# Ten instead of nine of 22 group products by seven multiplications in each half of a down projection

## The reference

```python
hf = rms_norm(x, norm_ffn)
gate, up = jnp.split(hf @ w_gu, 2, axis=-1)
return x + (jax.nn.silu(gate) * up) @ w_down      # [256 x 5632] @ [5632 x 2048]
```

## Time and profile before

| | before |
|---|---|
| time, median of 3 runs | 1106.16 us (1105.78 to 1106.39) |
| profiled execution | 1106.36 us, span 1104.6 us |
| TensorE matmul busy | 1092.2 us (99%), 5115 instructions |
| VectorE busy | 863.2 us (78%) |
| ScalarE busy | 580.2 us (53%) |
| down projection | about 865 to 1095 us of the span |
| granted TensorE clock | 0.997 of full speed on average |

### The profile page before, as it was taken

How to read it: one execution, slowest core, us unless ns; L and a number is a source line. 1 busy time by engine, 2 the same in 40 slices (tenths; PEclk the granted TensorE clock), 3 DMA queues, 4 the chain that set the end, 5 groups by cost and what they waited for, 6 DMA issues and landing times.

```text
span 1104.6 us, 13920 instructions
## 1 busy us (share of the span) xinstructions
PE 1092.2 (99%) x5115; PEld 908.8 (82%) x5115; DVE 863.2 (78%) x1057; ACT 580.2 (53%) x704; POOL 41.1 (4%) x70
## 2 busy tenths in 40 slices
PE   9999999999999999999999999999999999999996
PEld 7797889888888888888888888888888888888885
DVE  4556866688756557988988888889888898998895
ACT  4555545555445444545545545545455555656553
POOL 2600000000010000000000000000000000000000
PEclk9999999999999999999999999999999999999998
DMA  8665546565546675657557557566575866666663
GB/s 283 209 202 170 179 133 181 159 171 152 187 167 233 178 264 172 212 169 219 196 160 234 167 170 240 171 190 216 165 220 196 280 205 201 204 201 205 205 215 113
DMA packets 110637, 215.31 MB, mean 195 GB/s; under 512 B 6908, under 2 KB 11072, under 8 KB 109696
## 3 DMA queue, kind: packets, MB, share of 16 engines
q1 hardware_dynamic: 108960, 205.75, 59.9%
q0 software_dynamic: 1632, 8.96, 2.2%
HBM read 210.49 MB, written 4.19 MB: 194 GB/s over the span
## 4 chain that ended last, share of the span: by engine, by line
PE 93%; DVE 4%; DMA 1%; ACT 1%; issue 0%; POOL 0%; ACTq 0%; POOLq 0%; DVEq 0%
PE acc L1364 11%; PE acc L1635 11%; PE acc L1636 11%; PE acc L1637 11%; PE acc L1365 11%; PE acc L1366 11%; PE acc L1700 4%; PE acc L1701 4%; PE acc L1702 4%; PE mx L1356 2%; PE mx L1635 2%; PE mx L1636 2%; PE mx L1637 2%; DVE w_lo L1237 1%; PE mx L1700 1%; PE mx L1701 1%
## 5 line engine op out<-in xcount | busy, mean ns | idle before, releaser
L717 DVE TENSOR_TENSOR w_lo<-raw,w_hi 128x1024 fp32r<-128x1024 f32 (+2 forms) x144 | 166.6, 1170 | 117.9 <-ACT w_hi L430 117.2
L430 ACT ACTIVATE w_hi<-raw 128x1024 fp32r<-128x1024 f32 (+2 forms) x144 | 144.4, 1013 | 135.5 <-PE acc L1366 129.2
L618 ACT ACTIVATE w_hi<-raw 128x1024 fp32r<-128x1024 f32 (+1 forms) x160 | 158.4, 1005 | 94.8 <-PE acc L1637 81.1
L1635 PE MATMUL acc<-w_hi,hT_hi 128*128 128x512 f32 x520 | 203.3, 391 | 0.0
L1137 DVE TENSOR_TENSOR w_lo<-raw,w_hi 128x1024 fp32r<-128x1024 f32 (+1 forms) x160 | 180.5, 1154 | 29.1 <-ACT w_hi L618 27.3
L1636 PE MATMUL acc<-w_lo,hT_hi 128*128 128x512 f32 x520 | 202.4, 389 | 0.0
L1637 PE MATMUL acc<-w_hi,hT_lo 128*128 128x512 f32 x520 | 202.3, 389 | 0.0
L1364 PE MATMUL acc<-w_hi,hT_hi 128*128 128x512 f32 (+2 forms) x444 | 169.2, 381 | 0.3 <-DVE w_lo L717 0.3
L1366 PE MATMUL acc<-w_hi,hT_lo 128*128 128x512 f32 (+2 forms) x444 | 166.3, 375 | 0.0
L1365 PE MATMUL acc<-w_lo,hT_hi 128*128 128x512 f32 (+2 forms) x444 | 166.3, 375 | 0.0
L1637 PEld LDWEIGHTS acc<-w_hi,hT_lo 128*128 128x128 f32 x520 | 97.6, 188 | 20.4
(11 more groups left out here) (294 smaller groups left out, 1514.5 us busy)
## 6 DMA issues: line engine op xcount, KB each, us to landing
raw<-in_w_gu SPq DMA_DIRECT2D x176, 512.0 KB, 4.3
raw<-in_w_down SPq DMA_DIRECT2D x88, 512.0 KB, 4.7
raw<-in_w_in SPq DMA_DIRECT2D x80, 512.0 KB, 3.8
raw<-in_w_out SPq DMA_DIRECT2D x32, 512.0 KB, 4.5
raw<-in_w_in SPq DMA_DIRECT2D x8, 272.0 KB, 2.9
raw<-in_w_in SPq DMA_DIRECT2D x8, 264.0 KB, 2.8
tok<-in_x SPq DMA_DIRECT2D x8, 256.0 KB, 8.2
x<-in_x POOLq DMA_DIRECT2D x2, 1024.0 KB, 9.5
```

What stands on the lines that cost most here:

```text
L430: act.activation(w_hi[:, slot, 0:UC * width], raw[:, slot, 0:UC * width], ACT.Copy)\
L618: act.activation(w_hi[:, v % R, c0:UC * GW], raw[:, i % R, c0:UC * GW], ACT.Copy).then_inc(hi_ready, 1)
L717: dve.tensor_tensor(w_lo[:, slot, 0:UC * width], raw[:, slot, 0:UC * width], w_hi[:, slot, 0:UC * width].bitcast(F32), ALU.subtract).then_ ...
L1635: pe.matmul(o, a[0], w[0], start=first, stop=False)
```

## The change

In both halves group 18 becomes a seven, so there are ten sevens, eight pairs between them, and one place in each half where two sevens follow each other without a pair: behind the seventh seven (k=12) in half 0, behind the sixth (k=10) in half 1. The order becomes: half 0 pairs 1, 3, sevens 0 to 12 with pairs 5 to 15 between, seven 14, pair 17, seven 16, pair 19, seven 18, left 20, 21, right 20, 21; half 1 sevens 0 to 10 with pairs 1 to 9 between, seven 12, pair 11, seven 14, pair 13, seven 16, pair 15, seven 18, pair 17, then left and right 19, 20, 21. The last batch of `SPLIT` becomes groups 7 to 9 (three, not two). The last pass of gate and up makes summands too and is part of VectorE's loop. The tensors of summands grow by one group, and in SBUF the identity moves from the front to the end, behind the tensors of the late stages.

```diff
--- before.py
+++ after.py
@@ -85,7 +85,8 @@
 OUT_DONE = [U_OUT + max(i for i, (m, _k) in enumerate(OUT_ORDER) if m == n) + 1 for n in range(NG_OUT)]
 
 
-SUMMED = 9
+SUMMED = 10
+ADJACENT = (6, 5)
 
 
 def down_order():
@@ -93,13 +94,13 @@
     odd = [1, 3, 5, 7, 9, 11, 13, 15, 17, 19]
     for half in range(2):
         lead = odd[:2] if half == 0 else []
-        between = odd[len(lead):len(lead) + SUMMED - 1]
+        between = odd[len(lead):len(lead) + 8]
         rest = sorted(set(range(UPD)) - set(range(0, 2 * SUMMED, 2)) - set(lead) - set(between))
         groups = [("pair", k) for k in lead]
         for i in range(SUMMED):
             groups.append(("seven", 2 * i))
-            if i < SUMMED - 1:
-                groups.append(("pair", between[i]))
+            if i != ADJACENT[half] and between:
+                groups.append(("pair", between.pop(0)))
         alone = (2, LAST)[half]
         groups += [("pair", k) for k in rest[:-alone]]
         groups += [("left", k) for k in rest[-alone:]] + [("right", k) for k in rest[-alone:]]
@@ -141,7 +142,6 @@
             return sems[name]
 
 
-        ident = sb("ident", [P, P])
         cols = sb("cols", [P, 36])
         stat = sb("stat", [P, 96])
         ss_x, ms_x, rs_x = stat[:, 0:2], stat[:, 2:4], stat[:, 4:6]
@@ -200,22 +200,20 @@
         mixT_rows = scA[:, 0, :]
         early.close()
 
-        late = ExitStack()
-        actT_hi = sb("actT_hi", [P, FC, T], F32R, late, align=1024)
-        actT_lo = sb("actT_lo", [P, FC, T], F32R, late, align=1024)
-        gate_s = sb("gate_s", [P, NB, GW], where=late)
-        act_tok = sb("act_tok", [P, NB, GW], where=late)
-        s_lo = sb("s_lo", [P, SUMMED, 2, P], F32R, late, align=512)
-        up_s = sb("up_s", [P, NB, GW], where=late)
-        late.close()
-
-
         plain = ExitStack()
         actT_hi32 = sb("actT_hi32", [P, FC, T], F32, plain, align=1024)
         actT_lo32 = sb("actT_lo32", [P, FC, T], F32, plain, align=1024)
         sb("plain_gap", [P, 2 * NB, GW], F32, plain)
         s_32 = sb("s_32", [P, SUMMED, 2, P], F32, plain, align=512)
         plain.close()
+
+        actT_hi = sb("actT_hi", [P, FC, T], F32R, align=1024)
+        actT_lo = sb("actT_lo", [P, FC, T], F32R, align=1024)
+        gate_s = sb("gate_s", [P, NB, GW])
+        act_tok = sb("act_tok", [P, NB, GW])
+        s_lo = sb("s_lo", [P, SUMMED, 2, P], F32R, align=512)
+        up_s = sb("up_s", [P, NB, GW])
+        ident = sb("ident", [P, P])
 
 
         xin = tok[:, :, :].rearrange("p b n -> p (b n)")[:, 0:NB * D].rearrange("p (b n) -> p b n", b=NB)
@@ -1213,7 +1211,6 @@
             gate_up(1, True)
             with dve.Fori(2, SUMMED + 1) as j:
                 gate_up(j)
-            gate_up(SUMMED + 1, summed=False)
 
             def down_add(n, b, used):
 
```

## The result

The changed kernel takes 1114.2 us (median of 4, 1112.83 to 1116.44) against 1105.97 us before: ratio 1.0073, 95% interval 1.0061 to 1.0085. It is slower, by 8.2 us where 6.2 were forecast; the time lies near the upper end of the forecast range (1108.7 to 1114.4) and above the 1110.8 to 1113.8 given for the sum. The profiled execution took 1112.83 us, 6.5 us more than that of before.

The account below looks back on a forecast made before the run. TensorE's gapless matmul stream was taken to bound the kernel, with VectorE's small lead hidden behind it. Terms -1.36 + 3.34 + 3.2 + 0.5 + 0.2 + 0.3 = +6.2 us gave 1112.4 us, range 1108.7 to 1114.4.

Parts of the forecast that it names:

- six matmuls: In each half of the down projection one pair becomes a seven, 24 matmuls become 21; -1.36 us, counted in full.
- two couples of neighbours: Where two sevens follow each other, the second waits 1.67 us for VectorE's weight sums, twice; +3.34 us.
- join of the halves: Between half 0's last seven and half 1's first, four units cover VectorE's work instead of six; +3.2 us.
- third batch: Summands made behind the third seven grow from two groups to three, directly ahead of weight sums; +0.5 us.
- last pass: The final pass of gate and up now makes summands too, slowing its first seven; +0.2 us.
- end: Half 1's last seven is two units nearer the kernel's finish, so output additions come later; +0.3 us.
- place of the identity: Tensors move in SBUF but no instruction changes; 0, with 0.3 us either way.
- transfer late at k=12: Half 0's first neighbouring seven was late before; its own lateness may come or go by 0.7 us.
- rival D: After pauses at the join, the clock falls to 1.2 GHz for one period; 10.2 us more, 1122.6 us; chance 5%.
- A: Down projection waits stay hidden; only matmuls, summands and the last pass count; 1105.5 us; chance 8%.
- B: The join of the halves stays hidden and only the two neighbouring couples cost; 1109.2 us; chance 14%.
- C: Transfers issued late land after 5.7 us behind each of three waits, about 0.7 us each; 1114.5 us; chance 11%.

Follow-up runs that it names:

- the two neighbours alone: Kernel before, nine sevens, with half 1's pairs moved so the sevens of k=10 and k=12 follow each other; 1108.74 us against 1106.12, ratio 1.0022.
- the join with half 1 only: Changed kernel, but half 0 keeps its nine sevens and order, only half 1 has ten; 1108.53 us against 1106.12 before, ratio 1.0022.

## Why the prediction was right, and where its sizes were off

| term | forecast | in the traces |
|---|---|---|
| six matmuls | -1.36 | -1.36 |
| two couples of neighbours | +3.34 | +3.80 |
| join of the halves | +3.2 | +3.17 |
| third batch | +0.5 | +0.54 |
| last pass | +0.2 | +0.22 |
| end | +0.3 | +0.14 |
| place of the identity | 0 | not to be told from 0 |
| transfer late at k=12 | 0 | -0.84 in this execution |
| start and other passes | 0 | +0.64 in this execution |
| clock falling at the join | 5%, at +10.2 | 0 in this execution, +1.6 in the two later ones with a trace |

Without the last row the right column adds up to 6.3 us, where the spans differ by 6.4. The six terms that belong to the change (all but the last four rows) make 6.5 us, forecast 6.2. That the profiled execution came within 0.4 us of the forecast is in part luck: the transfer at k=12 was late only before, the start was late only after, and the two nearly cancel.

**What bounds.** The reading that a matmul stream without gaps hides a small lead held. The lead of 0.82 us at the seven's last slot is the same number in most periods of half 1, before and after; in a seven that comes late itself it is 0.57.

**Neighbours.** The chain (TensorE releases, ScalarE, low, sums, low, TensorE) was right to the step: 3.94 and 1.35 us came again. The sum was short by 0.12 us each, because the sums start 1.26 us after the last low does and not 1.14 (`weight_sums` waits for that low to be complete), and by 0.11 us each for the slow first matmul after a pause, which the earlier trace rows showed and I had not carried over.

**Join.** T+20.61 was forecast, T+20.59 measured; the first slot was forecast at T+16.99 by the same steps and came at T+16.97. It was the largest part that the words of the change do not mention.

**The missing 2 us.** The forecast of 1112.4 us was within 0.4 us of the profiled execution and 1.8 us below the median. The part of the prediction that was mis-sized is rival D. It was priced as one period at the lower level, 10.2 us, and given 5%; in the two traces that have it the fall lasts 3.4 us and costs 1.6, and by the mean clock it comes in about half of the executions, two of the first four among them. The rule of TensorE: Matmul & The Clock Gate in the Trainium skill (its decision table), that pauses between bursts bring the slow clock back, points the same way, but it is stated for longer pauses than these, so it does not predict this fall. The traces decide: the clock fell behind pauses of 0.9 and 2.1 us, and with these filled it held in the trace and, by the mean clock, in all five executions. The row that I set against it, a granted clock of 1.00 over a single pause of 0.7 us, did not resemble pauses this long and this close. One of the first four executions took 1114.02 us at a mean clock of 0.998; what made it late stays open.

**The other rivals.** A (hidden waits) is refuted by the two neighbours alone. B (a hidden join) is refuted by the 16.97 us in the trace, and the join with half 1 only shows that they come from half 0's order. C did not happen: no transfer was late behind a wait in the first profile. At k=12, ahead of the first couple, the lateness by a transfer varies from execution to execution, from nothing in the first profile to 0.8 us in the one with the pauses filled.

## What to carry to other kernels

Where one engine is busy without a gap, ask for the smallest lead of each engine that feeds it, and by whose release that lead is fixed; idle time ahead of such a release can't be used by work that is queued behind it, but it can by work moved ahead of it. Counting multiplications is not enough: a scheme that saves three of 24 matmuls here costs VectorE 6.7 us (2.66 for the sums, 4.0 for the lows) instead of 2.3, which needs a cheap neighbour on each side and at every join. And an added pause can have a second price beside its length, through the clock. Look at the granted clock behind it in more than one execution; here filling two pauses that lay close together, with work that computes nothing, paid.

## What the runs showed of the hardware

- After two pauses of 0.9 and 2.1 us, with 1.5 us of matmuls between them (984.26 to 985.76), the granted clock fell to 0.50 for 3.4 us in two of three traces, and by the mean clock in about half of 14 executions. Single pauses of 1.8 or 1.9 us (the neighbours) were not followed by a fall in any of the traces.
- The first matmul after a wait for VectorE is followed by the next after 0.30 to 0.34 us, not 0.227, at full granted clock.
- The clock's rise at the start differs from trace to trace, from 5.0 to 7.6 us of the span; TensorE's first product with weights starts at 9.10 us in the one and at 10.13 in the other, and everything behind it moves along.
